# The six modulation vectors of two layers, summed along the free axis with features on partitions

## The reference

```python
def ada_modulation(c, w, b):
    mod = jax.nn.silu(c) @ w + b                     # c (1, 1024), w (1024, 6144)
    return jnp.split(mod[:, None, :], 6, axis=-1)

def even_layer(x, c, ...):
    sh_m, sc_m, g_m, sh_f, sc_f, g_f = ada_modulation(c, ada_w, ada_b)
    h = rms_norm(x, norm_mix) * (1 + sc_m) + sh_m
    ...
    x = x + g_m * mix
    h = rms_norm(x, norm_ffn) * (1 + sc_f) + sh_f
    return x + g_f * swiglu(h, ffn_gate, ffn_up, ffn_down)
```

## Time and profile before

| | before |
|---|---|
| time, median of 3 runs | 1508.49 us (1505.85 to 1509.45) |
| profiled execution, time | 1511.99 us |
| its span, first to last instruction | 1510.2 us |
| PE busy | 1443.1 us, 96% |
| VectorE busy | 1220.9 us, 81% |
| ScalarE busy | 899.4 us, 60% |
| mean DMA rate | 236 GB/s |
| granted TensorE clock, mean | 0.987 |

### The profile page before, as it was taken

One profiled execution on the slowest core, in us unless ns is written; L12 is line 12 of the kernel. 1 busy time (PEld: TensorE's weight loads), 2 busy tenths in 40 slices (PEclk: granted clock), 3 DMA queues, 4 the chain that ended last, 5 costly groups with the idle time before them and its releaser, 6 DMA issues.

```text
span 1510.2 us, 19548 instructions
## 1 busy us (share of the span) xinstructions
PE 1443.1 (96%) x7128; PEld 1185.2 (78%) x7129; DVE 1220.9 (81%) x1664; ACT 899.4 (60%) x1207; POOL 5.6 (0%) x18
## 2 busy tenths in 40 slices
PE   6999999999999999998999999979899999999996
PEld 5888888887788887886788887856687888888885
DVE  6776879767767889878878788696688989999997
ACT  6555664556666563567433334446676877787764
POOL 0000000000000000000000000000000000000000
PEclk9999999999999999999999999979899999999999
DMA  8565446875355458561566786422289899898983
GB/s 295 230 227 191 167 169 235 336 265 221 112 205 186 154 181 305 212 240 59 205 262 256 268 311 231 167 84 85 112 326 343 317 330 325 341 355 328 335 325 138
DMA packets 53422, 356.15 MB, mean 236 GB/s; under 512 B 6096, under 2 KB 7120, under 8 KB 12896
## 3 DMA queue, kind: packets, MB, share of 16 engines
q1 hardware_dynamic: 52592, 352.15, 62.7%
q0 software_dynamic: 320, 2.65, 0.5%
q10 hardware_dynamic: 432, 0.30, 0.1%
HBM read 354.03 MB, written 1.05 MB: 235 GB/s over the span
## 4 chain that ended last, share of the span: by engine, by line
PE 76%; DVE 14%; ACT 5%; DMA 3%; issue 2%; SPq 0%; DVEq 0%; ACTq 0%
PE ps L447 23%; PE ps L449 22%; PE ps L448 22%; DVE wlo L1677 4%; DMA raw<-stream_dram 3%; PE ps L612 1%; ACT whi L1133 1%; DVE acc L1703 1%; PE ps L539 1%; PE ps L663 1%; PE ps L688 1%; DVE tok L1928 1%; ACT attn_scratch L1319 1%; PE ps L717 1%; DVE xlo L1767 1%
## 5 line engine op out<-in xcount | busy, mean ns | idle before, releaser
L1677 DVE TENSOR_TENSOR wlo<-raw,whi 128x2048 fp32r<-128x2048 f32 (+2 forms) x302 | 645.5, 2163 | 91.9 <-ACT whi L1133 78.4
L1133 ACT ACTIVATE whi<-raw 128x2048 fp32r<-128x2048 f32 (+2 forms) x302 | 541.8, 1817 | 183.1 <-DMA raw<-stream_dram 177.8
L447 PE MATMUL ps<-whi,xhi 128*128 128x512 f32 (+3 forms) x1360 | 534.0, 393 | 13.5 <-DVE xlo L2382 4.2
L449 PE MATMUL ps<-whi,xlo 128*128 128x512 f32 (+3 forms) x1360 | 522.6, 384 | 0.0
L448 PE MATMUL ps<-wlo,xhi 128*128 128x512 f32 (+3 forms) x1360 | 521.8, 384 | 0.0
L447 PEld LDWEIGHTS ps<-whi,xhi 128*128 128x128 f32 x1360 | 257.1, 189 | 70.2 <-issue 8.5
L449 PEld LDWEIGHTS ps<-whi,xlo 128*128 128x128 f32 x1360 | 256.9, 189 | 51.6
L448 PEld LDWEIGHTS ps<-wlo,xhi 128*128 128x128 f32 x1360 | 257.5, 189 | 46.7
L447 PE MATMUL ps<-whi,ahi 128*128 128x512 f32 x440 | 174.7, 397 | 3.7 <-DVE wlo L1677 2.5
L449 PE MATMUL ps<-whi,alo 128*128 128x512 f32 x440 | 171.7, 390 | 0.0
L448 PE MATMUL ps<-wlo,ahi 128*128 128x512 f32 x440 | 171.3, 389 | 0.0
(11 more groups left out here) (316 smaller groups left out, 1164.9 us busy)
## 6 DMA issues: line engine op xcount, KB each, us to landing
raw<-stream_dram SPq DMA_DIRECT2D x315, 1024.0 KB, 4.9
raw<-stream_dram SPq DMA_DIRECT2D x32, 512.0 KB, 4.7
attn_scratch<-toep_dram POOLq DMA_DIRECT2D x1, 2048.0 KB, 11.8
raw<-stream_dram SPq DMA_DIRECT2D x2, 528.0 KB, 4.4
h<-x_dram SPq DMA_DIRECT2D x2, 512.0 KB, 4.7
y<-tok SPq DMA_DIRECT2D x4, 256.0 KB, 2.6
head_scratch<-w_s_dram SPq DMA_DIRECT2D x1, 512.0 KB, 14.4
head_scratch<-vg_dram SPq DMA_DIRECT2D x1, 512.0 KB, 11.5
```

The source lines that it names most:

```text
L447: pe.matmul(o, xh, wh, start=start, stop=False)
L449: return pe.matmul(o, xl, wh, start=False, stop=stop)
L1133: act.activation(whi[:, q % SPL, 0:w], raw[:, s % RAW, 0:w], ACT.Copy).then_inc(sem("hi_done"), 1)
L1677: dve.tensor_tensor(low(q)[:, 0:w], raw[:, s % RAW, 0:w], whi[:, q % SPL, 0:w].bitcast(F32), ALU.subtract).then_inc(sem("lo_done"), 1)
```

## The change

The modulation slots are laid out the other way round: a slot now holds two blocks of 128 outputs, each output on its own partition with its 1024 weights along it. `c` comes as a row on all partitions (a new load of 512 KB on SP's queue behind slot 5), ScalarE applies Silu to the whole row in place, and one VectorE instruction for each block multiplies weights by the row, sums along it starting from the bias, and writes one column of `shf`, `scl` or `gcol`. So VectorE issues 2 instructions of 1024 elements a slot in place of 4 of 512. The matmuls of `ada_turn`, the taking of columns, `acc`, the waits for them and the holding back go; 1 + scale and gain are applied once, after a layer's last slot, in two small instructions. The 48 slots stand behind other weights. The descriptor buffer of POOL's loads is set to 8192 bytes.

```diff
@@ Plan.__init__
-        proj("gmlp_in", 2 * D, G_ORDER, layer=0, behind=(4, 5), first=FIRST)
-        proj("gmlp_out", D, layer=0, behind=odd)
+        proj("gmlp_in", 2 * D, G_ORDER, first=FIRST)
+        proj("gmlp_out", D, behind=(0, 1))
         proj("up0", 2 * FF)
-        proj("down0", D, kt=FK, layer=0, behind=(4, 5, 7, 8, 10, 11))
-        proj("kv", 2 * D, layer=0, behind=(2, 3, 5, 7))
-        proj("q", D, layer=0, behind=(1, 2))
-        proj("attn_out", D, layer=0, behind=odd)
+        proj("down0", D, kt=FK, behind=(1, 2, 3, 4, 6, 7, 8, 9))
+        proj("kv", 2 * D, behind=(2, 3, 5, 7))
+        proj("q", D, behind=(1,))
+        proj("attn_out", D, behind=(0, 1))
         proj("up1", 2 * FF)
-        proj("down1", D, kt=FK, layer=0, behind=(4, 5, 7, 8, 10, 11))
-        assert not left[0]
-        proj("e_in", E_IN, E_ORDER, layer=1, behind=(3, 5, 7, 8))
-        proj("e_out", D, layer=1, behind=odd)
-        proj("e_up", 2 * FF, layer=1, behind=odd[1:])
-        proj("e_down", D, kt=FK, layer=1, behind=(1, 2, 4, 5, 7, 8, 10, 11))
-        assert not left[1]
+        proj("down1", D, kt=FK, behind=(1, 2, 3, 4, 6, 7, 8))
+        assert len(self.ada) == ADA
+        proj("e_in", E_IN, E_ORDER, behind=(3, 5, 7))
+        proj("e_out", D, behind=(0, 1))
+        proj("e_up", 2 * FF, behind=odd)
+        proj("e_down", D, kt=FK, behind=(1, 2, 4, 5, 6, 7, 8, 9))
@@ sync
+                if s == 5:
+                    sp.dma_start(c_row[:, :], c_in.to_broadcast([P, D])).then_inc(sem("c_landed"), 16)
@@ tensor
-            def ada_turn(s):
-
-                if (s, turned[0] // (ADA // 2), 2 * (turned[0] % (ADA // 2)) + 1) not in PL.ada:
-                    return
-                if turned[0]:
-                    pe.wait_ge(sem("ada_taken"), turned[0])
-                pe.wait_ge(sem("lo_done"), s + 1)
-                for j in range(4):
-                    m = pe.matmul(ps[:, 4, j:j + 1], acc[:, j * P:(j + 1) * P], ones[:, 0:1], start=True, stop=True)
-                m.then_inc(sem("ada_cols"), 1)
-                turned[0] += 1
...
@@ gate_blocks
-                        pe.wait_ge(sem("ada_taken"), (layer + 1) * (ADA // 2))
                         n = T.up("gates") - 1
+                        pe.wait_ge(sem("modulated"), layer + 1)
@@ scalar
-                    act.activation(cs[:, :], cols[:, C_C:C_C + KT], ACT.Silu).then_inc(sem("cs"), 1)
+                    act.wait_ge(sem("c_landed"), 16)
+                    act.activation(c_row[:, :], c_row[:, :], ACT.Silu).then_inc(sem("cs"), 1)
@@ vector, modulate
                 dve.wait_ge(sem(f"landed{s % RAW}"), 16 * (s // RAW + 1))
-                for k in range(4):
-                    kk = 4 * (n % 2) + k
-                    wk = raw[:, s % RAW, k * W:(k + 1) * W]
-                    if kk == 0:
-                        m = dve.tensor_scalar(acc[:, :], wk, cs[:, 0:1], None, ALU.mult)
-                    else:
-                        m = dve.scalar_tensor_tensor(acc[:, :], wk, cs[:, kk:kk + 1], acc[:, :], ALU.mult, ALU.add)
-                    if k < 3 or n % 2 == 0:
-                        link(m)
...
+                for b in range(2):
+                    blk = 2 * n + b
+                    part, kind, k = blk // (3 * KT), blk // KT % 3, blk % KT
+                    wk = raw[:, s % RAW, b * D:(b + 1) * D]
+                    at = C_AB + layer * 6 * KT + blk
+                    m = dve.tensor_tensor_reduce(wk, wk, c_row[:, :], 1.0, cols[:, at:at + 1], ALU.mult, ALU.add,
+                                                 (shf2, scl2, gcol)[kind][:, layer, part, k:k + 1])
+                m.then_inc(sem("lo_done"), 1)
+                if seen[0] % ADA == 0:
+                    dve.wait_ge(sem("lo_done"), s + 1)
+                    for part in range(2):
+                        at = (C_GEM, C_GEF, C_GOM, C_GOF)[2 * layer + part]
+                        x = scl2[:, layer, part, :]
+                        m = dve.scalar_tensor_tensor(x, x, 1.0, cols[:, at:at + KT], ALU.add, ALU.mult)
+                    m.then_inc(sem("modulated"), 1)
@@ stream_of
-        w = a["e_ada_w_2" if layer == 0 else "o_ada_w_2"][0].reshape(KT, P, -1)
-        c = n // 2 * W
-        out[s] = w[4 * (n % 2):4 * (n % 2) + 4, :, c:c + W].transpose(1, 0, 2).reshape(P, SLOT)
+        w = a["e_ada_w_2" if layer == 0 else "o_ada_w_2"][0].reshape(D, -1, P)
+        out[s] = w[:, 2 * n:2 * n + 2, :].transpose(2, 1, 0).reshape(P, SLOT)
@@ kernel
-    nc = bacc.Bacc("TRN2", target_bir_lowering=False, num_devices=1)
+    nc = bacc.Bacc("TRN2", target_bir_lowering=False, num_devices=1, dynamic_dma_scratch_size=8192)
```

More of the change, by code:

```diff
@@ L107, in __init__, with add @@
         self.nq = 0
-        left = [ADA, ADA]
-        def add(widths, layer=None, behind=()):
+        def add(widths, behind=()):
             for i, w in enumerate(widths):
@@ L132, in proj @@
                 parts[0] = first
-            add([k * w for (_, w), ks in zip(chunks_of(n, order), parts) for k in ks], layer, behind)
+            add([k * w for (_, w), ks in zip(chunks_of(n, order), parts) for k in ks], behind)
         def expert():
@@ L828, in last_queries @@
                 pe.wait_ge(sem("tr_free"), T("tr"))
-            attention(CHUNKED, "attn_out", SM_C, PT_C, lead(2), between=last_queries)
+            attention(CHUNKED, SM_C, PT_C, lead(2), between=last_queries)
             gated_ffn(4, rest(3))
@@ L869, in _ @@
             proj(width[4], after=fox_heads)
-            attention(EVEN, "e_out", SM_E, PT_E, between=fox_keys)
+            attention(EVEN, SM_E, PT_E, between=fox_keys)
             gated_ffn(2, normed=True)
```

99 lines of the change are left out of this document (26 added, 73 removed).

## The result

The changed kernel takes 1500.05 us in the median (1496.87 to 1505.13), the kernel before 1507.22 in the same comparison; the ratio is 0.9949, with a 95% interval of 0.9937 to 0.9962. By the ratio that is 7.7 us or 0.5% faster (7.2 by the medians). The forecast was 1502.3 from 1508.49, a ratio of 0.9959. The profiled execution of the changed kernel took 1498.77 us with a span of 1497.0, 13.2 us less than the one of before.

What follows compares the result with a forecast made beforehand. TensorE's matmuls were taken as the bound (76% of the chain); -15.4 us for turns and the VectorE terms summed to -6.6, -6.2 after giving back 0.4: median 1502.3 us, own range 1498 to 1506, full range 1492 to 1512.

Steps and rivals of the forecast that it cites:

- A turn: Column-sum matmuls on TensorE: each of 24 displaces 0.81 us; 19 lie on the path, so removing them saves 15.4 us.
- The 0.4 that I gave back for e_in's attention: Just before e_in's attention: about 0.4 us of the saving lost again, because ScalarE's copies are close behind.
- The slot: VectorE's modulation work: two multiply-and-sum instructions at 1.20 us start to start, 2.4 us a slot, against 3.0 before.
- the rival of the half rate: Sums with both sources in SBUF run at half rate: 2.1 us more a slot, +36 us, 1538 us; chance 0.06.
- (a): gmlp_in and gmlp_out: two slots behind gmlp_out 0 and 1 make the casts of the next activations 0.4 us later.
- (b): down0: three slots stand in VectorE's chain without idle time, so TensorE gets an awaited low-half tile 4.2 us later.
- (c): down1: the same queueing on VectorE as in down0, +4.0 us; 1.4 us come back at the normalisation behind it.
- (d): Attention: the second slot delays low parts, +0.7 us in attn_out, +0.3 in e_out; -0.9 at e_out's normalisation.
- (e): e_down: slots without a break free buffers late, about 1 and 1.8 us at weights 7 and 8; net +1.6 us.
- (f): kv and q lose 0.1 us of a turn; e_in and e_up lose none, TensorE being without a gap there.
- The queue costs more than TensorE saves: VectorE's queue in the down projections eats the gain: 1507 to 1516 us, say 1511, slower or no gain; chance 0.28.
- The queue is shorter than I count: Down-projection slots cost little and the removed column sums come through whole: 1493 us; chance 0.12.

## Why the prediction was right, and where it was not

The forecast was right, and so was its mechanism: TensorE gives its turns, and VectorE's queue in the down projections takes half of it back. By its steps, as the starts of the weight tiles show them:

- **A turn** was mis-sized. I priced it at 0.81 us, from the start of the matmul ahead of it to that of the one behind it. The differences of before and after say 0.79 to 0.90 at the next matmul, mostly 0.82 or 0.85, and behind most of those with 0.82 another 0.13 over the matmuls that follow. A turn of down0 in the trace before shows both:

```profile
256.09 0.40 PE L449 MATMUL ps<-whi,alo 128*128 128x512 f32 x1
256.32 0.95 PE L663 MATMUL ps<-ones,acc 128*128 128x1 f32 x8
257.13 0.48 PE L447 MATMUL ps<-whi,ahi 128*128 128x512 f32 x1
257.45 0.39 PE L448 MATMUL ps<-wlo,ahi 128*128 128x512 f32 x1
```

  The first matmul behind the turn is itself slower: 0.32 us to the next start instead of 0.23, and the twelve of that tile take 2.86 us where they take 2.72 after the change. The earlier trace rows had the matmul of 0.48 us; I stopped one row too soon. And the turn at 359.6, which I had called eaten by a slot but for 0.2, gave its 0.8: the lead of 1.91 us behind it is whole at attn_out's start (390.82 to 388.91). The steps in the differences that are turns add up to 18.0 us, 20 turns at 0.90, where I had 19 at 0.81 and the 0.2, 15.6. With 2.4 more the sum is -9.0 at the start of o_in, where the traces show -9.1 (0.3 of which stands there before any step, in the first tiles). The 0.4 that I gave back for e_in's attention was not there: the difference is -3.39 ahead of it and -3.36 behind.
- **The slot** at 2.4 us held: 2.41, and 1279 ns a sum (1.27 forecast). 128x1024 elements with a sum take 1279 ns, as long as the 1285 ns of the earlier trace rows without one, so the rival of the half rate fell. The Trainium skill, Vector Engine (DVE) Microarchitecture Reference, section "Points that are easy to get wrong", gives half throughput to a scalar-tensor-tensor instruction with two sources in SBUF that aren't bf16. Neither of these two rows shows it; whether the page means the sum as well, which the trace records as an instruction of another name, is open.
- **(a)** +0.40 in gmlp_out (0.4 forecast).
- **(b)** +4.17 in down0 (4.2), **(c)** +3.97 in down1 (4.0), with the waits at weights 3, 4 and 5: 4.3 us of idle time in down0, 4 to 5 forecast. In front of e_in -1.30 (-1.4).
- **(d)** +0.66 in attn_out (0.7), +0.35 in e_out (0.3), -0.8 in front of e_up (-0.9).
- **(e)** +0.94 and +1.68 before weights 7 and 8 (1 and 1.8), -0.9 in front of o_in (-1.0). The run with small loads bears out the way that I gave for weight 7, from the use of weight 4 over landing, copy and split. One figure in it was off: a whole tile's matmuls take 5.44 us (885.12 to 890.56 in the trace before, weights 4 and 5), not 5.7. Against 5.44 + 2.72 for weights 5 and 6 my 9.1 leaves 0.94, all of the measured step, where I had 0.6 and put the rest down to waits.
- **(f)** kv, q, e_in and e_up moved by their turns and by nothing else that is over 0.1 us.
- **The rivals.** "The queue costs more than TensorE saves" needed a slot of 2.8 us. "The queue is shorter than I count" fell with the waits above. What it would have given, 1493, is about what the old places give (1490.83).
- **What would show it.** TensorE's busy time came to 1422.5 (near 1424).

The terms agree to a tenth or two, the turn apart. That the time itself was met so well, -6.2 forecast and -7.2 to -7.7 measured, is in part luck: the turns gave 2.4 us more and the 0.4 was not given back, and 1.6 us that no step of mine had went again in o_in, by the clock. What the experiments put right is of another kind: I held that turns taken from the path are worth their length. Alone they were worth 12 us by the ratio and 14.5 by the trace at o_in, not 18. The largest of the losses, 1.2 us, is at the normalisation behind down1, through which VectorE, kept back by landings, doesn't follow TensorE. In the change this stayed hidden, because the new places clear VectorE's queue in front of just these. And I took the last places of a down projection for harmless in my expectations, where late slots cost 3 to 4 us in front of the next projection. Of the 3.8 us lost by e_down at its old places the transfer has 2.25 and the lower clock 0.76, and 0.8 stay open; for down1 that it is the transfer is argued from this, not tested. Why the clock falls stays open too. In all six places where it fell ahead of a projection's first matmul at the ends of down1, e_out and e_down, TensorE had been idle just before (2.17 to 4.44 us), but it was idle for 2.54 behind down1 in the run without turns and the clock stayed high, and in o_in it fell with TensorE busy, for 3.4 us in one kernel and for 6.8 in another.

## What to carry to other kernels

Price an instruction that goes by the starts of its neighbours on both sides, one matmul further than seems needed. Before moving work on an engine that is not the bound, list for every tile how long it is ready before it is used, and put the work where this slack is longer than the work: here that was worth 19 us on top of the change's 7.7, and the change had used 7.4 us of it up. Look at three queues for each place, as they gave three different costs: the engine's own order (2.4 us a slot in a chain without a gap), the buffer that comes free late (1 to 2 us a tile), and the transfer that delays what is awaited behind the stage (2.3 us in e_down, with 0.8 more where TensorE's clock falls while it waits).

## What the runs showed of the hardware

- A multiply-and-sum of VectorE over 128x1024 fp32, both sources in SBUF, takes 1279 ns, over 128x8 it takes 222; the next one starts 1.21 us after it with the 82 ns read of the sum hidden, and 1.33 us after it when each has to complete first.
- Eight passes of fp32 matmuls with a single column displace 0.82 us of a stream of 128x512 matmuls, and the first of these behind them is 0.09 us slower (0.32 us to the next start for 0.23, kernel before, 257.13).
- Eight matmuls of 128x256 took 1.89 us at the full clock and 3.34 with a granted clock of 0.50 (changed kernel and e_down at its old places, in front of o_in).
- A megabyte of weights took 4.8 us from the end of the matmuls that freed its buffer until ScalarE started on it, with the slots' loads an eighth as large (881.28 to 886.08) and at full size (881.65 to 886.42) alike.
- With identical code the expert stage, up to its last weight tile, took 407.3 to 413.4 us from one profiled execution to another: a difference of 13 us between two traces is no measure of a change, that of the starts up to a common point is.
